# Two weight panels at a time behind a norm, and a residual's scaling moved among the next panels

## The chip, the cores and the metric

The kernel runs on one core of a Trainium2 chip. The time is the device time of one execution in microseconds (us). Three executions of the kernel before took 3048.42, 3040.75 and 3049.32 us; their median is 3048.42.

## What is computed

Two small language-model blocks run one behind the other on one sequence of 512 tokens of width 1024. The first has two layers, each a mixer (a linear recurrence with gated linear attention, then a forgetting attention) and an MLP, joined by layer norms; the second has two hybrid layers (three kinds of attention side by side, then a gated feed-forward), joined by RMS norms. What matters here is what stands around each norm:

```python
# first block, for both layers
x = layer_norm(ALPHA * x + gate * y, ln_g[layer, 0], ln_b[layer, 0])
shift, scale, gate = ada_mod(c, ada_w[layer, 1], ada_b[layer, 1])
u = x * (1.0 + scale) + shift
y = jnp.square(jax.nn.relu(u @ mlp_w1[layer] + mlp_b1[layer])) @ mlp_w2[layer] + mlp_b2[layer]
x = layer_norm(ALPHA * x + gate * y, ln_g[layer, 1], ln_b[layer, 1])

# second block, for both layers
h = rms_norm_2(x, norm_mix) * (1 + sc_m) + sh_m
... = jnp.split(h @ w_in, points, axis=-1)        # then the mixer
h = rms_norm_2(x, norm_ffn) * (1 + sc_f) + sh_f
gate, up = jnp.split(h @ w_gate_up, 2, axis=-1)
return x + gt_f * ((jax.nn.silu(gate) * up) @ w_down)
```

## The kernel before

**Layout.** Activations lie transposed: a matrix of 1024 features by 512 tokens is 8 tiles of 128 partitions by 512. `X` (residual) holds x. A product's input is kept as two tiles in the fast fp32 matmul format, `UHI` (in_high, the rounded value) and `ULO` (in_low, what rounding left). A weight panel is 1024 rows by 128 columns (512 KB) and is likewise split into `WHI` and `WLO`. `gemm` (from L585) multiplies one panel with all 8 input tiles into one PSUM bank: for each tile three matmuls of 128x512, high by high, high by low input, low weight by high (L596 to L598), so 24 for a panel. Products alternate between banks 0 and 1, and a product may start once the product two before it has been read out of its bank.

**Weights.** SyncE streams all panels in the order of use into a ring of 4 slots. ScalarE makes the high part (`high`, L1717), VectorE the low part (`low`, L1092), into 3 split slots; a slot is free when the matmuls of the panel three before are done. `prepare(ahead(key))` stands ahead of each panel's own work on both engines and splits the panels up to the second one after it. Among the MLP's panels the stream also holds rows of the modulation matrices ("ada"), about one a panel, which VectorE multiplies and sums (L1101).

**A norm.** PE sums the squares (or centred squares) with a constant matrix; ScalarE takes the inverse root into `R`, which is the first of two `tmp` tiles (L1759, L1762). Then `norm_split` makes the next product's input, tile by tile, for k = 0 to 7: VectorE scales X[k] into a stage tile (L1185), ScalarE adds the shift and rounds to in_high (L1800), VectorE takes what is left as in_low (L1182). The first panel behind the norm waits for in_low of each tile in turn (the `ready` argument of `gemm`); the second panel starts when the first has ended. There are seven such places: three layer norms (0 and 2 ahead of an MLP, 1 ahead of the forgetting attention) and, in both hybrid layers, an RMS norm ahead of the mixer and one ahead of the feed-forward. 

**Behind a layer norm** VectorE then scales all 8 tiles of the residual itself with gain and R (L1175) before it goes on to the MLP's panels. ScalarE's first step in the MLP waits for that (`s.wait_ge(*at("ln_norm", i - 1, KT - 1))`), since it writes the first panel's result into the tile that R lies in; it waits there before `evict`, so also before it splits the next weight panel. In the MLP each of the 16 panels of a half goes: ScalarE adds the bias and takes relu (L1731), VectorE squares (L1212), ScalarE rounds (L1810), VectorE takes the low part (L1202).

The order on each engine is the order of the calls in `tensor_program`, `vector_program` and `scalar_program`; semaphores alone tie them together.

## Time and profile before

| | us |
|---|---|
| median of three executions | 3048.42 (3040.75 to 3049.32) |
| the profiled execution, its own time | 3052.84 |
| its span, first to last instruction | 3051.4 |
| PE (TensorE matmul) busy | 2859.7, 94% of the span |
| VectorE (DVE) busy | 1673.2, 55% |
| ScalarE (ACT) busy | 1121.3, 37% |
| mean granted TensorE clock | 0.962 of full |

In the profile PE is the matmul unit and PEld its weight load, which runs beside it; L596 is line 596 of the kernel before. A timeline row gives start, duration, engine, line, operation, output<-inputs, and in brackets the idle time before it and what ended that. The duration of a matmul includes its way through the array: successive matmuls overlap, and the distance from start to start is what each costs. The granted clock is a share of full speed; PE has two levels, 1.2 and 2.4 GHz, so a mean of 0.9 over a stretch is a fifth of its time at the low one.

### The profile page before, as it was taken

Reading aid. Unit: us, or ns where it says so; the run is one execution under the profiler, and the core shown is the slowest. Engines: PE = TensorE matmul, PEld = TensorE weight load, DVE = VectorE, ACT = ScalarE, POOL = GpSimd, SP = SyncE. Lnnn points to the kernel's source line nnn. Section 1 sums busy time; section 2 is a strip of 40 time slices with the busy share of each in tenths; the row PEclk is TensorE's granted clock in tenths of the full one; section 3 lists DMA queues with packets and bytes.
Section 4 is the critical chain, followed back from the end, with each engine's and each line's share of the span. In section 5 each row is a group of like instructions: output and inputs, shape, how many; then the busy total and the mean of one; then the engine's idle time right before and its main releaser. Section 6 shows DMA issues by size and latency. Waiting matters only on the chain.

```text
span 3051.4 us, 35357 instructions
## 1 busy us (share of the span) xinstructions
PE 2859.7 (94%) x14106; PEld 2287.4 (75%) x14106; DVE 1673.2 (55%) x2910; ACT 1121.3 (37%) x1908; POOL 9.4 (0%) x21
## 2 busy tenths in 40 slices
PE   5888999989998899997999989999989899899998
PEld 4666888866666688875887867888868778678887
DVE  6678646554555755655547655443545476543334
ACT  3444324234554433324435333222334343332223
POOL 0000000000000000000000000000000000000000
PEclk9999999999998999998989899999999999999999
DMA  6345555522221465642220013444422100122222
GB/s 238 117 135 169 191 168 186 192 98 70 70 70 57 137 207 180 206 152 82 90 76 1 1 42 118 138 148 136 163 95 100 51 1 1 62 84 97 97 97 83
DMA packets 92067, 336.19 MB, mean 110 GB/s; under 512 B 10480, under 2 KB 10736, under 8 KB 91776
## 3 DMA queue, kind: packets, MB, share of 16 engines
q1 hardware_dynamic: 86800, 315.40, 30.7%
q10 hardware_dynamic: 3792, 14.31, 1.3%
q0 software_dynamic: 1312, 4.23, 0.5%
q8 instruction: 113, 1.85, 0.2%
q14 instruction: 50, 0.41, 0.0%
HBM read 331.76 MB, written 2.13 MB: 109 GB/s over the span
## 4 chain that ended last, share of the span: by engine, by line
PE 87%; DVE 7%; ACT 4%; DMA 1%; issue 1%; ACTq 0%; DVEq 0%
PE bank L596 22%; PE bank L597 22%; PE bank L598 22%; PE bank L781 2%; PE bank L795 2%; PE bank L770 2%; PE bank L1014 1%; DVE in_low L1182 1%; DVE hidden L1185 1%; PE bank L869 1%; PE bank L613 1%; PE bank L614 1%; PE bank L644 1%; PE bank L615 1%; PE bank L1022 1%; PE bank L1025 1%
## 5 line engine op out<-in xcount | busy, mean ns | idle before, releaser
L596 PE MATMUL bank<-in_high,weights_high 128*128 128x512 f32 x2160 | 874.6, 405 | 49.5 <-DVE in_low L1182 36.6
L597 PE MATMUL bank<-in_low,weights_high 128*128 128x512 f32 x2160 | 854.9, 396 | 0.0
L598 PE MATMUL bank<-in_high,weights_low 128*128 128x512 f32 x2160 | 854.2, 395 | 0.0
L1092 DVE TENSOR_TENSOR weights_low<-weight_ring,weights_high 128x1024 fp32r<-128x1024 f32 x404 | 494.1, 1224 | 469.8 <-ACT weights_high L1717 469.7
L1717 ACT ACTIVATE weights_high<-weight_ring 128x1024 fp32r<-128x1024 f32 x404 | 424.6, 1051 | 473.4 <-PE bank L598 320.6
L596 PEld LDWEIGHTS bank<-in_high,weights_high 128*128 128x128 f32 x2160 | 413.9, 192 | 186.1 <-issue 55.5
L598 PEld LDWEIGHTS bank<-in_high,weights_low 128*128 128x128 f32 x2160 | 413.8, 192 | 89.0
L597 PEld LDWEIGHTS bank<-in_low,weights_high 128*128 128x128 f32 x2160 | 414.9, 192 | 85.3 <-issue 4.1
L596 PE MATMUL bank<-hidden_split,weights_high 128*128 128x512 f32 x864 | 336.1, 389 | 0.0
L597 PE MATMUL bank<-hidden_split,weights_high 128*128 128x512 f32 x864 | 336.1, 389 | 0.0
L598 PE MATMUL bank<-hidden_split,weights_low 128*128 128x512 f32 x864 | 336.1, 389 | 0.0
L1101 DVE CUSTOM_DVE_ANT_0 weight_ring<-weight_ring,silu_c,vectors 128x1024 f32<-128x1024 f32 x192 | 244.4, 1279 | 3.4 <-DMA weight_ring<-stream 3.3
L596 PEld LDWEIGHTS bank<-hidden_split,weights_high 128*128 128x128 f32 x864 | 162.2, 188 | 33.8
L598 PEld LDWEIGHTS bank<-hidden_split,weights_low 128*128 128x128 f32 x864 | 162.2, 188 | 33.8
L597 PEld LDWEIGHTS bank<-hidden_split,weights_high 128*128 128x128 f32 x864 | 162.2, 188 | 33.5
L1810 ACT ACTIVATE hidden_split<-tmp 128x512 fp32r<-128x512 f32 x108 | 68.4, 633 | 262.5 <-DVE tmp L1546 205.5
L1731 ACT ACTIVATE tmp<-bank 128x512 f32<-128x512 f32 (+1 forms) x77 | 46.0, 597 | 245.1 <-PE bank L598 245.1
L1927 ACT ACTIVATE probs<-probs,columns 128x256 f32<-128x256 f32 (+4 forms) x144 | 73.7, 513 | 167.1 <-DVE columns L1346 164.8
L1202 DVE TENSOR_TENSOR hidden_split<-tmp,hidden_split 128x512 fp32r<-128x512 f32 x108 | 74.8, 693 | 75.5 <-ACT hidden_split L1810 75.5
L1546 DVE TENSOR_TENSOR tmp<-bank,tmp 128x512 f32<-128x512 f32 x44 | 30.4, 692 | 118.2 <-PE bank L598 118.2
L1731 ACT ACTIVATE tmp<-bank,vectors 128x512 f32<-128x512 f32 (+1 forms) x65 | 44.6, 686 | 136.2 <-PE bank L598 136.2
L781 PE MATMUL bank<-probs_T,hidden 128*64 128x128 f32 (+1 forms) x816 | 71.5, 302 | 24.4 <-DVE probs_T L1376 24.2
(332 smaller groups left out, 2961.4 us busy)
## 6 DMA issues: line engine op xcount, KB each, us to landing
weight_ring<-stream SPq DMA_DIRECT2D x597, 512.0 KB, 3.4
mixer_out<-cmp ACTq DMA_DIRECT2D x6, 1024.0 KB, 4.8
hidden<-forget_rows POOLq DMA_DIRECT2D x16, 256.0 KB, 3.8
residual<-x ACTq DMA_DIRECT2D x4, 512.0 KB, 12.7
mixer_out<-cmp SPq DMA_DIRECT2D x2, 1024.0 KB, 6.3
out<-mixer_out ACTq DMA_DIRECT2D x4, 512.0 KB, 2.7
constants<-consts ACTq DMA_DIRECT2D x1, 2013.5 KB, 21.0
silu_c<-c ACTq DMA_DIRECT2D x2, 512.0 KB, 4.6
```

The source lines that it names most:

```text
L596: pe.matmul(bank[:, :], WHI[:, z, cols], high, start=(k == 0), stop=False)
L597: pe.matmul(bank[:, :], WHI[:, z, cols], low, start=False, stop=False)
L598: ins = pe.matmul(bank[:, :], WLO[:, z, cols], high, start=False, stop=(k == ktiles - 1))
L770: pe.matmul(B[2 + z][:, 0:w], it["q"], it["k"], start=True, stop=True).then_inc(*mark("tensor_attention", *name, "scores", 2 * d + z))
L781: ins = pe.matmul(it["out"], it["v"][c], turned[:, blk(c)], start=it["start"] and c == 0, stop=it["stop"] and c == m - 1, skip_group_check ...
L1092: v.tensor_tensor(WLO[:, z, :], ring[:, n % RING, :], WHI[:, z, :].bitcast(F32), ALU.subtract).then_inc(*mark("weights_low", "low", n))
L1101: v.tensor_tensor_reduce(w, w, SC[:, :], 1.0, vec1("ada_b", col, col + 1), ALU.mult, ALU.add, MODS[:, col:col + 1]).then_inc(*mark("modula ...
L1202: v.tensor_tensor(HSPLIT[:, 1, at_, :], tmp, HSPLIT[:, 0, at_, :].bitcast(F32), ALU.subtract).then_inc(*mark("vector_mlp", *event))
L1717: s.activation(WHI[:, i % NSPLIT, :], ring[:, n % RING, :], ACT.Copy).then_inc(*mark("weights_high", "high", n))
L1731: s.activation(dst, view(B_of(key)[:, :]), func, **kw).then_inc(*mark("scalar_evict", "evicted", key))
L1810: s.activation(HSPLIT[:, 0, at_, :], tmp, ACT.Copy).then_inc(*mark("scalar_mlp", *event))
L1927: s.activation(p, p, ACT.Exp, bias=nm, scale=-1.0, accum_out=COL[:, c + 2 + z:c + 3 + z]).then_inc(*mark(sem, *name, "exp", i))
```

## The change

A new `gemm_pair` multiplies two panels with the same input tiles, into two banks. It waits at its start for both panels' low parts, then takes tile k for the first panel and tile k-2 for the second, in turns, waiting for in_low of tile k only ahead of the first panel's three matmuls. It stands behind six of the seven norms: for the first two "up" panels of each MLP, the first two rotary panels of each mixer, and the first gate and up panel of each feed-forward. The panel behind layer norm 1 stays as it was.

For layer norms 0 and 2 the inverse root goes to `M[:, 7, :]` instead of R, ScalarE no longer waits for `ln_norm` in the MLP, and the eight scalings of the residual are issued one at a time behind the first eight panels of the MLP's first half (`ln_scale`). Layer norms 1 and 3 keep theirs.

```diff
@@ -398,6 +398,8 @@
     ident, ones = const("ident"), const("ones")
     EPS = {1e-5: const("eps")[:, 0:1], 1e-6: const("eps")[:, 1:2]}
     R = TMP[:, 0, 0:T]
+
+    ln_root = lambda i: M[:, 7, :] if i in (0, 2) else R
     LNG, LNS, RB = (COL[:, 88 + 8 * z:96 + 8 * z] for z in range(3))
     blk = lambda b: slice(b * P, b * P + P)
     chunk = lambda c: slice(c * 64, c * 64 + 64)
@@ -600,6 +602,26 @@
                 ins.then_inc(*mark("panels_used", "used", n))
             ev.also("panels_used", "gemm", key)
 
+        def gemm_pair(keys, x, ready):
+
+            banks, used = [gemm_bank(key) for key in keys], [PANELS[key][0] for key in keys]
+            for n in used:
+                pe.wait_ge(*at("low", n))
+            for k in range(KT + 2):
+                for bank, n, j in zip(banks, used, (k, k - 2)):
+                    if not 0 <= j < KT:
+                        continue
+                    if j == k:
+                        pe.wait_ge(*at(*ready(k)))
+                    z, cols = split_turn[n] % NSPLIT, slice(j * P, j * P + P)
+                    high, low = x(j)
+                    pe.matmul(bank[:, :], WHI[:, z, cols], high, start=(j == 0), stop=False)
+                    pe.matmul(bank[:, :], WHI[:, z, cols], low, start=False, stop=False)
+                    ins = pe.matmul(bank[:, :], WLO[:, z, cols], high, start=False, stop=(j == KT - 1))
+                    if j == KT - 1:
+                        ins.then_inc(*mark("panels_used", "used", n))
+                        ev.also("panels_used", "gemm", keys[used.index(n)])
+
         def gemm_tok(name, panels, per, width, event, banks):
 
             for i in range(panels):
@@ -660,8 +682,10 @@
 
         def mlp(l, i):
             for half in range(2):
-                for j in range(HALF):
-                    gemm(("up", l, half, j), u_split, ready=lambda k: ("norm_out", "ln", i - 1, k) if (half, j) == (0, 0) else None)
+                if half == 0:
+                    gemm_pair([("up", l, 0, 0), ("up", l, 0, 1)], u_split, lambda k: ("norm_out", "ln", i - 1, k))
+                for j in range(2 if half == 0 else 0, HALF):
+                    gemm(("up", l, half, j), u_split)
                 for m in range(KT):
                     gemm(("down", l, half, m), h_split, HALF, ready=lambda k: hidden_ready(("up_low", l, half), HALF, k) if m == 0 else None)
             ln_mean(i)
@@ -872,8 +896,9 @@
 
             conv = lambda m: gemm(("conv", l, m), u_split)
             z = lambda m: gemm(("z", l, m), u_split)
-            gemm(ropes[0], u_split, ready=lambda k: ("norm_out", "mix", l, k))
-            for i in range(1, 5):
+            gemm_pair(ropes[0:2], u_split, lambda k: ("norm_out", "mix", l, k))
+            turn(0)
+            for i in range(2, 5):
                 gemm(ropes[i], u_split)
                 turn(i - 1)
             gemm(("kc", l), u_split)
@@ -945,8 +970,11 @@
             for a in range(0, FF2_T, HALF):
                 tiles = min(HALF, FF2_T - a)
                 for j in range(a, a + tiles):
-                    gemm(("gate", l, j), u_split, ready=lambda k: ("norm_out", "ffn", l, k) if j == 0 else None)
-                    gemm(("gup", l, j), u_split)
+                    if j == 0:
+                        gemm_pair([("gate", l, 0), ("gup", l, 0)], u_split, lambda k: ("norm_out", "ffn", l, k))
+                    else:
+                        gemm(("gate", l, j), u_split)
+                        gemm(("gup", l, j), u_split)
                 for m in range(KT):
                     gemm(("fdown", l, a, m), h_split, tiles, 
                                ready=lambda k: hidden_ready(("gup_low", l), tiles, k, a) if m == 0 else None)
@@ -1170,19 +1198,23 @@
                 v.wait_ge(*last("modulations"))
             v.wait_ge(*at("ln_r", i))
             if mod is not None:
-                norm_split(("ln", i), lambda k: LNG[:, k:k + 1], lambda k: LNS[:, k:k + 1])
-            for k in range(KT):
-                v.scalar_tensor_tensor(X[:, k, :], X[:, k, :], gcol_[:, k:k + 1], R, ALU.mult, ALU.mult).then_inc(
-                    *mark("vector_norm", "ln_norm", i, k))
-
-        def norm_split(event, gain, shift):
+                norm_split(("ln", i), lambda k: LNG[:, k:k + 1], lambda k: LNS[:, k:k + 1], ln_root(i))
+            if i in (1, 3):
+                for k in range(KT):
+                    ln_scale(i, k, gcol_)
+
+        def ln_scale(i, k, gcol_):
+            v.scalar_tensor_tensor(X[:, k, :], X[:, k, :], gcol_[:, k:k + 1], ln_root(i), ALU.mult, ALU.mult).then_inc(
+                *mark("vector_norm", "ln_norm", i, k))
+
+        def norm_split(event, gain, shift, root):
 
             def tile_low(k):
                 v.wait_ge(*at("norm_high", *event, k))
                 v.scalar_tensor_tensor(ULO[:, k, :], H[:, STAGE + k, :], shift(k), UHI[:, k, :].bitcast(F32), ALU.add,
                                        ALU.subtract).then_inc(*mark("vector_norm", "norm_out", *event, k))
             for k in range(KT):
-                v.scalar_tensor_tensor(H[:, STAGE + k, :], X[:, k, :], gain(k), R, ALU.mult, ALU.mult).then_inc(
+                v.scalar_tensor_tensor(H[:, STAGE + k, :], X[:, k, :], gain(k), root, ALU.mult, ALU.mult).then_inc(
                     *mark("vector_norm", "norm_scaled", *event, k))
                 if k:
                     tile_low(k - 1)
@@ -1190,7 +1222,7 @@
 
         def rms_norm(event, gain, shift):
             v.wait_ge(*at("rms_r", *event))
-            norm_split(event, lambda k: gain[:, k:k + 1], lambda k: shift[:, k:k + 1])
+            norm_split(event, lambda k: gain[:, k:k + 1], lambda k: shift[:, k:k + 1], R)
 
         def input_low(k, src, high, event):
             v.wait_ge(*at(*high))
@@ -1211,6 +1243,8 @@
                     v.wait_ge(*at("evicted", key))
                     v.tensor_tensor(h, h, h, ALU.mult).then_inc(*mark("vector_mlp", "up_square", l, half, j))
                     hidden_low(j, h, ("up_high", l, half, j), ("up_low", l, half, j))
+                    if half == 0 and j < KT:
+                        ln_scale(i - 1, j, vec1("ln_g", 8 * i - 8, 8 * i))
                 if half == 0:
                     gb = COL[:, 72:80]
                     v.wait_ge(*last("modulations"))
@@ -1785,7 +1819,7 @@
                 s.wait_ge(*at("ln_centre", i, k))
                 s.activation(M[:, k, :], X[:, k, :], ACT.Square).then_inc(*mark(sem, "ln_square", i, k))
             s.wait_ge(*at("ln_var", i, KT - 1))
-            inv_sqrt(sem, B[3], 1e-5, R, ("ln_r", i))
+            inv_sqrt(sem, B[3], 1e-5, ln_root(i), ("ln_r", i))
             if mod is not None:
                 s.wait_ge(*at("ln_shift", i))
                 norm_high(("ln", i), LNS)
@@ -1815,8 +1849,6 @@
                     h = TMP[:, j % 2, 0:T]
                     if j > 1:
                         s.wait_ge(*at("up_low", l, half, j - 2))
-                    elif j == 0 and half == 0:
-                        s.wait_ge(*at("ln_norm", i - 1, KT - 1))
                     b1 = 32 * l + HALF * half + j
                     evict(("up", l, half, j), h, ACT.Relu, bias=vec1("mlp_b1", b1, b1 + 1))
                     s.wait_ge(*at("up_square", l, half, j))
```

On PE, at the MLP behind layer norm 0, the matmuls of input tiles 2 and 3 (bank0 is the first panel's, bank1 the second's; "vector_norm" is the wait for in_low). Before:

```order
L596 MATMUL bank0<-in_high_49,weights_high 128x512 [waits vector_norm]
L597 MATMUL bank0<-in_low,weights_high 128x512
L598 MATMUL bank0<-in_high_49,weights_low 128x512
L596 MATMUL bank0<-in_high_49,weights_high 128x512 [waits vector_norm]
L597 MATMUL bank0<-in_low,weights_high 128x512
L598 MATMUL bank0<-in_high_49,weights_low 128x512
```

Now:

```order
L618 MATMUL bank0<-in_high_49,weights_high 128x512 [waits vector_norm]
L619 MATMUL bank0<-in_low,weights_high 128x512
L620 MATMUL bank0<-in_high_49,weights_low 128x512
L618 MATMUL bank1<-in_high_49,weights_high 128x512
L619 MATMUL bank1<-in_low,weights_high 128x512
L620 MATMUL bank1<-in_high_49,weights_low 128x512
L618 MATMUL bank0<-in_high_49,weights_high 128x512 [waits vector_norm]
```

Between two tiles of the first panel there now stand three matmuls of the second.

On VectorE, at the same place, from the last two in_low tiles on (L1101 or L1129 is a modulation row, "ISA" its two parts; weights_low the next panel's low part; tmp and hidden_split the first panel's square and low part). Before:

```order
L1182 SCALAR_TENSOR_TENSOR in_low<-hidden,columns,in_high_49 128x512 [waits scalar_norm] x2
L1175 SCALAR_TENSOR_TENSOR residual<-residual,vectors1,tmp 128x512 x8
L1101 ISA weight_ring,modulations<-weight_ring,silu_c,vectors1 128x1024 [waits panel_landed_0]
L1101 ISA modulations 128x1
L1092 TENSOR_TENSOR weights_low<-weight_ring,weights_high 128x1024 [waits weights_high]
L1212 TENSOR_TENSOR tmp<-tmp 128x512 [waits scalar_evict]
L1202 TENSOR_TENSOR hidden_split_51<-tmp,hidden_split_51 128x512 [waits scalar_mlp]
```

Now:

```order
L1214 SCALAR_TENSOR_TENSOR in_low<-hidden,columns,in_high_49 128x512 [waits scalar_norm] x2
L1129 ISA weight_ring,modulations<-weight_ring,silu_c,vectors1 128x1024 [waits panel_landed_0]
L1129 ISA modulations 128x1
L1120 TENSOR_TENSOR weights_low<-weight_ring,weights_high 128x1024 [waits weights_high]
L1244 TENSOR_TENSOR tmp<-tmp 128x512 [waits scalar_evict]
L1234 TENSOR_TENSOR hidden_split_51<-tmp,hidden_split_51 128x512 [waits scalar_mlp]
L1207 SCALAR_TENSOR_TENSOR residual<-residual,vectors1,mixer_out 128x512
L1129 ISA weight_ring,modulations<-weight_ring,silu_c,vectors1 128x1024 [waits panel_landed_2]
```

The eight scalings are gone from behind the last in_low, and one stands behind the low part of each of eight panels.

On ScalarE, at the same place, the last in_high tiles and the MLP's first steps. Before:

```order
L1800 ACTIVATE in_high_49<-hidden,columns 128x512 [waits vector_norm] x7
L1717 ACTIVATE weights_high<-weight_ring 128x1024 [waits panels_used,panel_landed_1,vector_norm]
L1731 ACTIVATE tmp<-bank0,vectors1 128x512 [waits panels_used]
L1810 ACTIVATE hidden_split_51<-tmp 128x512 [waits vector_mlp]
L1717 ACTIVATE weights_high<-weight_ring 128x1024 [waits panels_used,panel_landed_3]
```

Now:

```order
L1834 ACTIVATE in_high_49<-hidden,columns 128x512 [waits vector_norm] x7
L1751 ACTIVATE weights_high<-weight_ring 128x1024 [waits panels_used,panel_landed_1]
L1765 ACTIVATE tmp<-bank0,vectors1 128x512 [waits panels_used]
L1844 ACTIVATE hidden_split_51<-tmp 128x512 [waits vector_mlp]
L1751 ACTIVATE weights_high<-weight_ring 128x1024 [waits panels_used,panel_landed_3]
```

The order is the same; the high part of the third panel has lost its wait for VectorE ("vector_norm").

## Rows read from the trace of the kernel before

**Rows 1.** The page: busy time of PE and of its weight load

```profile
PE 2859.7 (94%) x14106; PEld 2287.4 (75%) x14106; DVE 1673.2 (55%) x2910; ACT 1121.3 (37%) x1908; POOL 9.4 (0%) x21
```

**Rows 2.** Waits over the whole span: us in total, times, longest

```profile
PE bank L596 <- DVE in_low L1182: 36.6, 25, 7.3
```

**Rows 3.** Timeline of PE, first MLP: first panel, second panel, start of the third

```profile
266.96 0.47 PE L596 MATMUL bank<-in_high,weights_high 128*128 128x512 f32 x1 [4.00 <-DVE in_low L1182]
...
268.19 0.71 PE L596 MATMUL bank<-in_high,weights_high 128*128 128x512 f32 x1 [0.30 <-DVE in_low L1182]
...
269.54 0.77 PE L596 MATMUL bank<-in_high,weights_high 128*128 128x512 f32 x1
270.11 0.63 PE L597 MATMUL bank<-in_low,weights_high 128*128 128x512 f32 x1
270.53 0.63 PE L598 MATMUL bank<-in_high,weights_low 128*128 128x512 f32 x1
...
274.81 0.50 PE L596 MATMUL bank<-in_high,weights_high 128*128 128x512 f32 x1 [0.36 <-DVE in_low L1182]
...
275.69 0.50 PE L596 MATMUL bank<-in_high,weights_high 128*128 128x512 f32 x1
...
276.49 0.40 PE L596 MATMUL bank<-in_high,weights_high 128*128 128x512 f32 x1
...
281.72 0.39 PE L598 MATMUL bank<-in_high,weights_low 128*128 128x512 f32 x1
283.44 0.47 PE L596 MATMUL bank<-in_high,weights_high 128*128 128x512 f32 x1 [1.33 <-DVE weights_low L1092]
```

**Rows 4.** Timeline of VectorE at the same place

```profile
272.69 0.75 DVE L1182 SCALAR_TENSOR_TENSOR in_low<-hidden,columns,in_high 128x512 fp32r<-128x512 f32 x1
...
274.01 1.62 DVE L1182 SCALAR_TENSOR_TENSOR in_low<-hidden,columns,in_high 128x512 fp32r<-128x512 f32 x2
275.56 5.38 DVE L1175 SCALAR_TENSOR_TENSOR residual<-residual,vectors,tmp 128x512 f32<-128x512 f32 x8
280.86 1.28 DVE L1101 CUSTOM_DVE_ANT_0 weight_ring<-weight_ring,silu_c,vectors 128x1024 f32<-128x1024 f32 x1
...
282.07 1.23 DVE L1092 TENSOR_TENSOR weights_low<-weight_ring,weights_high 128x1024 fp32r<-128x1024 f32 x1
```

**Rows 5.** Timeline of ScalarE at the same place

```profile
274.13 0.72 ACT L1800 ACTIVATE in_high<-hidden,columns 128x512 fp32r<-128x512 f32 x1 [0.60 <-DVE hidden L1185]
280.97 1.06 ACT L1717 ACTIVATE weights_high<-weight_ring 128x1024 fp32r<-128x1024 f32 x1 [6.12 <-DVE residual L1175]
281.94 0.67 ACT L1731 ACTIVATE tmp<-bank,vectors 128x512 f32<-128x512 f32 x1
```

**Rows 6.** Six windows, from the first panel's start to the third's; last columns clock, DMA, GB/s

```profile
266.96:283.44 16.48, 14.12 (x48) 9.34 (x49) 16.35 (x25) 5.98 (x8) 0.00 (x0) 0.90 0.02 5
1008.17:1024.66 16.49, 13.94 (x48) 9.25 (x49) 16.36 (x25) 5.98 (x8) 0.00 (x0) 0.90 0.01 3
1395.44:1410.43 14.99, 14.63 (x48) 10.28 (x49) 9.78 (x14) 5.90 (x8) 0.00 (x0) 0.80 0.10 37
1849.87:1864.85 14.98, 14.45 (x48) 10.15 (x49) 12.20 (x17) 8.13 (x10) 0.00 (x0) 0.81 0.24 76
2223.13:2238.12 14.99, 14.16 (x48) 9.80 (x49) 9.78 (x14) 5.89 (x8) 0.00 (x0) 0.85 0.10 35
2675.85:2690.84 14.99, 14.48 (x48) 10.16 (x49) 11.01 (x15) 8.12 (x10) 0.00 (x0) 0.81 0.19 56
```

**Rows 7.** Timeline of PE in the first product, which takes four banks in turn

```profile
31.05 0.40 PE L631 MATMUL bank<-in_high,weights_low 128*128 128x512 f32 x1
31.29 0.39 PE L629 MATMUL bank<-in_high,weights_high 128*128 128x512 f32 x1
31.52 0.39 PE L630 MATMUL bank<-in_low,weights_high 128*128 128x512 f32 x1
```

**Rows 8.** Timeline of VectorE among the MLP's later panels

```profile
322.52 0.69 DVE L1212 TENSOR_TENSOR tmp<-tmp 128x512 f32<-128x512 f32 x1 [1.01 <-ACT tmp L1731]
```

**Rows 9.** PE's waits from the third panel to the next norm's sums (window 283.4 to 625)

```profile
PE bank L644 <- ACT mixer_out L1786: 1.4, 1, 1.4
```

## The prediction

> **What bounds the kernel now.** I read the page's busy times first: PE works for 94% of the span [rows 1], so time can only come from the places where it stands still or runs slow. The list of waits names the one that this change is about: 36.6 us in 25 waits for in_low of a norm [rows 2]. Not all of it can go. Seven of the waits, one for each norm, are the wait for the first tile (4.00 us at the first MLP [rows 3]); the chain of sums, root and first tile ahead of it is not touched. What can go stands behind the first tile, and for that I read the three engines' timelines at the first MLP.
>
> The input's tiles come every 1.32 us: two in_low on VectorE start at 272.69 and 274.01 [rows 4], since between them stands the next tile's scaling. A tile of one panel costs PE three matmuls. The starts of successive ones are 0.42 to 0.43 us apart at the low clock (270.11 to 270.53 [rows 3]) and 0.23 at the full one (31.29 to 31.52 [rows 7]; 0.227 over the 24 matmuls from 276.49 to the end 0.23 behind the start at 281.72 [rows 3], 5.45 us a panel). So at the low clock a tile costs 1.28 us and PE is just filled; at full clock it costs 0.68 and PE waits about half the time, as at 274.81 [rows 3]. The first panel thus ends at 276.49 and only then does the second begin, with all its input there. That is the second panel's 5.45 us, nearly all of it behind the last tile.
>
> At the MLPs there is a second loss. VectorE scales the residual for 5.38 us from 275.56 [rows 4]; ScalarE waits for that for 6.12 us before it splits the third panel's high part [rows 5], VectorE's modulation row and low part follow [rows 4], and PE, done with the second panel at 281.95, starts the third at 283.44 [rows 3]: 1.49 us.
>
> **The change, part by part.** *The pair.* Tiles 0 and 1 go as before. From tile 2 on, each tile brings six matmuls: 1.36 us at full clock, more than the 1.32 between tiles, and 2.56 at the low one. So from there PE should not wait again. What is left of the 48 matmuls is 42, or 42 x 0.227 = 9.53 us at full clock. Tile 2 begins 2.58 us behind tile 0 at the first MLP (269.54 less 266.96 [rows 3]); I take 2.6 at all six. Each us of low clock behind that point costs 1 - 0.227/0.427 = 0.47 us. The low clock's length is in the windows' granted clock [rows 6], each window running from the first panel's start to what follows the second: twice (1 - clock) times the length. That gives 3.3 us at both MLPs, 6.0, 5.7, 4.5 and 5.7 at the other four. At the first MLP PE had run the first tile at full clock and was slow from tile 1 (0.43 between starts from 269.54 on, and by 276.49 long fast [rows 3]), so 3.3 us end some 1.9 behind tile 2; I take that at both. At the others the first matmuls are already slow, and 3.4, 3.1, 1.9 and 3.1 us lie behind tile 2.
>
> The pair's end, counted from the first start: 2.6 + 9.53 + 0.47 x slow = 13.0 at the MLPs, and 13.7, 13.6, 13.0 and 13.6 at mixer, feed-forward, mixer, feed-forward. Against the window lengths of 16.48, 16.49, 14.99, 14.98, 14.99 and 14.99 [rows 6] that is 3.46, 3.47, 1.26, 1.38, 1.97 and 1.39 us less: together 12.9. The MLPs' figures take in the 1.49 us wait each, which the next step has to earn.
>
> *The scaling moved.* VectorE ends its last in_low at about 275.6, the modulation row and the low part (1.28 and 1.23 [rows 4]) then end at 278.1. ScalarE is free for the high part from 274.9 [rows 5]. The pair ends at about 280.0, so the third panel is ready 1.9 us early, and the 1.49 us go. The fourth panel is the tight one. The first panel ends at about 278.0 (three tiles, 2.04 us, ahead of the pair's end). From there: eviction 0.7, square 0.7, high part 0.7, low part 0.7, the moved scaling 0.67 (5.38/8), modulation row 1.28, weights' low part 1.2: about 6.1 us, done at 284.1; PE asks for it at 280.0 + 5.45 = 285.5. It is 1.4 us early. Later VectorE does 4.3 us of that chain plus 0.67 for each 5.45 us panel, and it idles 1.01 us in each before the square [rows 8], so eight scalings fit.
>
> *What costs nothing.* The pair needs both panels' low parts and both banks at its start; all four were ready long before, since VectorE splits the second panel while the projection ahead still runs, and cover is the 4 us wait for the first tile itself. The banks change every three matmuls: the first product does so with four banks at 0.23 us a start [rows 7]. The root in a `mixer_out` tile is written and read in the same lengths. Behind the pair PE meets no wait for weights up to the next norm's sums, one of 1.4 us for a square apart [rows 9], so nothing is in place to take the gain back, and everything behind is shifted as it stands.
>
> The Trainium skill's page "TensorE: Matmul & The Clock Gate" (section "Back-to-back issue gap") gives 216 ns for a matmul of 512 columns at full clock; the rows show 227. By the page's figure each pair would end 42 x 0.011 = 0.46 us sooner, an estimate of 2.8 us more in all; the measurement decides and the sum stays.
>
> **The sum** is 12.9 us. Bounds: with no slow stretch at all behind tile 2 the six pairs give 2.8 us each (14.99 - 2.6 - 9.53) and the MLPs' waits 3.0, near 20; with the low clock 2 us longer at each and the MLPs' waits staying, 12.9 - 5.6 - 3.0 = 4.3. From the profiled execution's 3052.84 this makes 3039.9, from the median of 3048.42 it makes 3035.5. A change of 0.3% is 9.1 us; that is about what a measurement can tell from none here, the three runs lying 8.6 us apart.
>
> **The rivals.** *A: a new wait in the MLP.* If the fourth panel comes late (a ring slot landing late, or ScalarE and VectorE waiting for each other once more than in my chain), PE waits there, and since each of eight panels carries one scaling, the moved 5.4 us could come back one by one. For it: only 1.4 us of margin. Against: 1.01 us of idle a panel [rows 8], and low parts that are done nearly two panels ahead once PE is the slower. Price: the MLPs give 1 to 2 us each in place of 3.5, total gain 8, 3040: within 0.3%.
>
> *B: the low clock lasts longer in the pair.* PE would drain the backlog at 0.43 a matmul. Two us more at each place cost 5.6: gain 7, 3041. Against it: PE was already filled at the low clock before, so what it does up to the clock's rise is the same.
>
> *C: it ends earlier,* as the windows differ by 1.5 us among themselves [rows 6]: gain 16 to 19, 3031.
>
> *D, slower.* The pair changes banks every three matmuls; if that broke the stream into pieces, the clock could stay low for the whole pair: 42 x 0.427 = 17.9 in place of 9.5, an end at 20.5. Against 15.0 and 16.5 that loses 5.5 us at four places and 4.0 at two, 30 us: 3078. It decides from 4.6 us more low clock at each place (12.9/6/0.47). Against it: four banks in turn ran at full clock [rows 7]. The same page (section "A second HAM failure mode: psum-queue depth-cycling") tells of a kernel in which cycling through PSUM banks let the clock swing between its levels; there PE idled between groups. The trace shows the cycling without the swing.
>
> *E: nothing shows,* as the gain is within what runs differ by.
>
> **How the numbers follow.** My forecast (gain 10 to 16) has 0.70, A 0.10, B 0.08, C 0.06, D 0.03, E 0.03. Faster by over 0.3% takes the forecast and C: 0.76; within 0.3% A, B and E: 0.21; slower 0.03. The time is the forecast's 3035.5. The range takes in 6 us of gain at one end (A and B) and 19 at the other (C), 3029 to 3043.
>
> **What would show it.** Right: at six places, the matmuls of the pair without a wait from tile 2 on, the third panel's start 13.0 to 13.7 us behind the first's in place of 15.0 to 16.5; waits of PE for in_low down by about 4 us (the starts behind the first tile); ScalarE's 6.12 us wait for the residual gone; no wait of PE for weights_low at the MLPs. Wrong: L596's successor waiting for weights_low or a ring transfer in the MLP's panels 3 to 10 (A), starts 0.43 us apart past 6 us behind the first (B, D), or the gain present at the six places and the same time found as new waits before the end.

## The result

Nine executions of each: the changed kernel took 3026.02 us in the median (3023.30 to 3035.70), the kernel before 3046.57 (3036.19 to 3049.57). The medians lie 20.6 us apart; the ratio of the executions is put at 0.9945, 95% interval 0.993 to 0.996, which is 17 us less (12 to 21). A second comparison, six executions against 25, gave 3030.43 us in the median and 0.9951 (0.9932 to 0.9969), 15 us less. Faster, as forecast, by somewhat more than the 12.9 us of the sum; the first median lies 3 us under the low end of the range.

The profiled execution has a span of 3024.3 us against 3051.4. The page's busy times, and PE's waits over the whole span (answering to [rows 1, 2]):

```profile
PE 2842.2 (94%) x14106; PEld 2279.3 (75%) x14106; DVE 1672.9 (55%) x2910; ACT 1122.6 (37%) x1908; POOL 9.4 (0%) x21
```

```profile
PE bank L618 <- DVE in_low L1214: 27.3, 8, 6.9
...
PE bank L598 <- DVE in_low L1214: 5.0, 4, 4.0
```

Waits for in_low fell from 36.6 to 32.3 us. What is left is the first tile's at seven places, and little more: the six pairs (L618) have 8 waits in all.

PE at the first MLP (answering to [rows 3]):

```profile
265.39 0.47 PE L618 MATMUL bank<-in_high,weights_high 128*128 128x512 f32 x1 [4.00 <-DVE in_low L1214]
...
268.07 0.68 PE L618 MATMUL bank<-in_high,weights_high 128*128 128x512 f32 x1
...
269.40 0.59 PE L618 MATMUL bank<-in_high,weights_high 128*128 128x512 f32 x1
269.82 0.40 PE L619 MATMUL bank<-in_low,weights_high 128*128 128x512 f32 x1
...
278.49 0.39 PE L598 MATMUL bank<-in_high,weights_high 128*128 128x512 f32 x1
```

Tile 2 starts at 268.07 and no matmul waits from there to the third panel (L598), which starts at 278.49, 13.10 us behind the first, where it was 16.48.

VectorE and ScalarE there (answering to [rows 4, 5]):

```profile
272.45 1.63 DVE L1214 SCALAR_TENSOR_TENSOR in_low<-hidden,columns,in_high 128x512 fp32r<-128x512 f32 x2
274.00 1.28 DVE L1129 CUSTOM_DVE_ANT_0 weight_ring<-weight_ring,silu_c,vectors 128x1024 f32<-128x1024 f32 x1
...
275.21 1.22 DVE L1120 TENSOR_TENSOR weights_low<-weight_ring,weights_high 128x1024 fp32r<-128x1024 f32 x1
...
279.37 0.75 DVE L1207 SCALAR_TENSOR_TENSOR residual<-residual,vectors,mixer_out 128x512 f32<-128x512 f32 x1
...
281.24 1.22 DVE L1120 TENSOR_TENSOR weights_low<-weight_ring,weights_high 128x1024 fp32r<-128x1024 f32 x1
282.38 0.69 DVE L1244 TENSOR_TENSOR tmp<-tmp 128x512 f32<-128x512 f32 x1
```

```profile
273.20 1.04 ACT L1751 ACTIVATE weights_high<-weight_ring 128x1024 fp32r<-128x1024 f32 x1
276.65 0.69 ACT L1765 ACTIVATE tmp<-bank,vectors 128x512 f32<-128x512 f32 x1 [2.40 <-PE bank L620]
```

ScalarE's 6.12 us wait is gone. The third panel's low part is done at 276.4, 2.1 us early; the fourth's at 282.5, where PE asks for it at 278.49 + 5.45 = 283.9: 1.5 us early.

The six windows, from the first panel's start to what follows the pair (answering to [rows 6]; the last three columns are clock, DMA share, GB/s):

```profile
265.39:278.49 13.10, 12.80 (x49) 9.91 (x49) 11.60 (x17) 6.39 (x9) 0.00 (x0) 0.87 0.14 48
1006.24:1019.24 13.00, 12.70 (x49) 9.90 (x49) 11.59 (x17) 6.39 (x9) 0.00 (x0) 0.87 0.17 45
1389.90:1402.25 12.35, 12.35 (x49) 9.79 (x50) 9.78 (x14) 5.91 (x8) 0.00 (x0) 0.88 0.10 28
1834.18:1847.87 13.69, 13.69 (x48) 10.72 (x49) 11.25 (x17) 8.14 (x10) 0.00 (x0) 0.79 0.17 48
2205.76:2218.11 12.35, 12.35 (x49) 9.75 (x50) 9.78 (x14) 5.91 (x8) 0.00 (x0) 0.89 0.10 32
2650.00:2663.71 13.71, 13.71 (x48) 10.71 (x49) 10.05 (x15) 8.13 (x10) 0.00 (x0) 0.79 0.12 39
```

The places gain 3.38, 3.49, 2.64, 1.29, 2.64 and 1.28 us: 14.7 in all. The two spans differ by 27.1. Where the other 12 came from is the question of half the experiments. Most of them lie in stretches of the hybrid layers that hold no changed instruction. A first guess was that they are therefore not the change's; that does not follow yet, since a change can alter what comes behind it.

### The profile page after: what moved, and what is told of

The parts are those of the page before. It is cut to its first block, busy times and chain, and to the rows that moved or that the text cites. A ratio compares the mean times of both kernels' runs of the same rounds, so it can differ in the third digit from the quotient of the medians.

```text
span 3024.3 us, 35357 instructions
## 1 busy us (share of the span) xinstructions
PE 2842.2 (94%) x14106; PEld 2279.3 (75%) x14106; DVE 1672.9 (55%) x2910; ACT 1122.6 (37%) x1908; POOL 9.4 (0%) x21
## 4 chain that ended last, share of the span: by engine, by line
PE 89%; DVE 5%; ACT 4%; DMA 1%; issue 1%; ACTq 0%; DVEq 0%
PE bank L598 22%; PE bank L599 22%; PE bank L600 22%; PE bank L819 2%; PE bank L794 2%; PE bank L805 2%; PE bank L1042 1%; PE bank L635 1%; PE bank L1050 1%; PE bank L893 1%; PE bank L636 1%; PE bank L666 1%; PE bank L637 1%; PE bank L618 1%; PE bank L1053 1%
## 5 line engine op out<-in xcount | busy, mean ns | idle before, releaser
L598 PE MATMUL bank<-in_high,weights_high 128*128 128x512 f32 x2064 | 826.3, 400 | 15.4 <-DVE in_low L1229 7.4
L600 PE MATMUL bank<-in_high,weights_low 128*128 128x512 f32 x2064 | 812.4, 394 | 0.0
L599 PE MATMUL bank<-in_low,weights_high 128*128 128x512 f32 x2064 | 811.7, 393 | 0.0
L598 PEld LDWEIGHTS bank<-in_high,weights_high 128*128 128x128 f32 x2064 | 393.2, 190 | 128.7 <-issue 24.0
L599 PEld LDWEIGHTS bank<-in_low,weights_high 128*128 128x128 f32 x2064 | 392.8, 190 | 83.4 <-issue 4.1
L600 PEld LDWEIGHTS bank<-in_high,weights_low 128*128 128x128 f32 x2064 | 392.1, 190 | 83.5
L598 PE MATMUL bank<-hidden_split,weights_high 128*128 128x512 f32 x864 | 336.1, 389 | 0.0
L1129 DVE CUSTOM_DVE_ANT_0 weight_ring<-weight_ring,silu_c,vectors 128x1024 f32<-128x1024 f32 x192 | 244.5, 1279 | 3.7 <-DMA weight_ring<-stream 3.6
L598 PEld LDWEIGHTS bank<-hidden_split,weights_high 128*128 128x128 f32 x864 | 162.2, 188 | 33.7
```

Source lines behind the costliest of these rows:

```text
L598: pe.matmul(bank[:, :], WHI[:, z, cols], high, start=(k == 0), stop=False)
L599: pe.matmul(bank[:, :], WHI[:, z, cols], low, start=False, stop=False)
L600: ins = pe.matmul(bank[:, :], WLO[:, z, cols], high, start=False, stop=(k == ktiles - 1))
L1129: v.tensor_tensor_reduce(w, w, SC[:, :], 1.0, vec1("ada_b", col, col + 1), ALU.mult, ALU.add, MODS[:, col:col + 1]).then_inc(*mark("modula ...
```

## The experiments

The experiments ran on three chips, each beside the kernel before on the same chip. Its medians there were 3045.50, 3042.70 and 3048.36 us, so whole times are compared by ratios to it, or within one chip. Five kernels ran once, for their trace, and are read by their stages.

**The two parts apart.** The scaling moved, without pairs:

```diff
         def gemm_pair(keys, x, ready):
+            gemm(keys[0], x, ready=ready)
+            gemm(keys[1], x)
+
+        def gemm_pair_unused(keys, x, ready):
```

> The scaling moved and ScalarE's wait gone, but the first two panels one after the other at all seven norms. Both theories of the change's parts: the third panel at the two MLPs starts 15.0 us behind the first (16.48 before, 13.0 to 13.1 with the whole change), since its low part is ready before the second panel ends; the four hybrid places stay at 15.0. Gain 1.5 us at each MLP, 3.0 in all, so within 0.1 to 0.2% of the kernel before. If the changed kernel's surplus over its six places (27 us in span against 14.7 us at the places) came from the moved scaling, this one would be 12 us or more faster as well.

The pairs, with the scaling as before:

```diff
-    ln_root = lambda i: M[:, 7, :] if i in (0, 2) else R
+    ln_root = lambda i: R
...
-            if i in (1, 3):
-                for k in range(KT):
+            for k in range(KT):
...
-                    if half == 0 and j < KT:
-                        ln_scale(i - 1, j, vec1("ln_g", 8 * i - 8, 8 * i))
...
+                    elif j == 0 and half == 0:
+                        s.wait_ge(*at("ln_norm", i - 1, KT - 1))
```

> The six pairs, but with the scaling in one piece behind the norm, the root in the tmp tile and ScalarE's wait as before. Theory of the two parts needing each other at the MLPs: VectorE ends the scaling and the third panel's low part at the same time as before, so the third panel still starts 16.4 to 16.5 us behind the first and the MLPs gain nothing, though the pair ends at 13.1; the four hybrid places give 5 to 8 us by how long the low clock lasts. Total gain 5 to 8 us from the places. Rival (the parts add up independently): third panel at 14.6 behind the first, 1.9 us at each MLP, total 9 to 12.

PE at the first MLP, first tile and third panel, with the scaling moved:

```profile
264.66 0.47 PE L598 MATMUL bank<-in_high,weights_high 128*128 128x512 f32 x1 [4.00 <-DVE in_low L1218]
...
279.65 0.39 PE L598 MATMUL bank<-in_high,weights_high 128*128 128x512 f32 x1
```

and with the pairs alone:

```profile
263.39 0.47 PE L618 MATMUL bank<-in_high,weights_high 128*128 128x512 f32 x1 [4.00 <-DVE in_low L1213]
...
276.15 0.39 PE L620 MATMUL bank<-in_high,weights_low 128*128 128x512 f32 x1
279.87 0.47 PE L598 MATMUL bank<-in_high,weights_high 128*128 128x512 f32 x1 [3.33 <-DVE weights_low L1120]
```

14.99 and 16.48 us, as expected of both. The pair alone ends 13.0 us behind its start (276.15 + 0.23) and then waits 3.33 us for the weights: at the MLPs it is worth nothing without the moved scaling, which alone is worth 1.5, and together they give 3.4 to 3.5. Over the whole, the scaling moved gave 0.9992 (0.9975 to 1.0009), which 3.0 us at its two places fit and 12 us would not, and the pairs alone 0.9976 (0.9961 to 0.9991), 7 us, with 7.6 at its four hybrid places. The rival for each is out.

**How much margin the moved scaling has.** Two more scalings beside each of the eight, whose results are not read:

```diff
                     if half == 0 and j < KT:
+                        for d in range(2):
+                            v.scalar_tensor_tensor(M[:, 3 + d, :], X[:, j, :], vec1("ln_g", 8 * i - 8 + j, 8 * i - 7 + j),
+                                                   ln_root(i - 1), ALU.mult, ALU.mult).then_inc(*step("vector_norm"))
                         ln_scale(i - 1, j, vec1("ln_g", 8 * i - 8, 8 * i))
```

> The changed kernel with two more scalings of the same size (their results are not read) beside each of the eight in each MLP. It measures the margin of the moved scaling. By the trace of the changed kernel VectorE takes 5.00 us for a panel with one scaling while it catches up, PE 5.45; each further scaling adds 0.67. Theory 'VectorE's chain is the only limit': 6.3 us a panel, 0.9 over PE's, the fourth panel's low part has 1.5 us of margin and loses 1.3 of it at once, so PE waits in each of the following panels by up to 0.9 us: 5 to 7 us in each MLP, first wait of PE for weights_low at the fourth or fifth panel. Rival 'low parts are made far ahead, there is ample cover': no wait of PE, the MLP takes 365.7 us as with one scaling.

From one norm's sums to the next, the first MLP took 370.9 us in place of 365.8 and the second 372.0 in place of 365.7, 5.1 and 6.3 more. PE's waits from 262 to 380:

```profile
PE bank L598 <- DVE weights_low L1120: 3.4, 6, 0.6
```

and VectorE's low parts of the first and second panel's output, with the two added scalings (L1248) between them:

```profile
278.73 0.69 DVE L1234 TENSOR_TENSOR hidden_split<-tmp,hidden_split 128x512 fp32r<-128x512 f32 x1 [0.70 <-ACT hidden_split L1847]
279.33 1.41 DVE L1248 SCALAR_TENSOR_TENSOR mixer_out<-residual,vectors,mixer_out 128x512 f32<-128x512 f32 x2
...
285.05 0.69 DVE L1234 TENSOR_TENSOR hidden_split<-tmp,hidden_split 128x512 fp32r<-128x512 f32 x1 [0.70 <-ACT hidden_split L1847]
```

VectorE's round for a panel takes 6.32 us (278.73 to 285.05), its 0.70 us of waiting for ScalarE included; with one scaling it took 5.01 (277.37 to 282.38 in the changed kernel). PE meets six waits in the first MLP, the first at the fifth panel, and its panels then start 6.32 us apart instead of 5.44. So the limit of the moved scaling is reached when VectorE's round for a panel passes PE's 5.45. The single execution took 3035.98 us.

**The lag.** Both panels on the same tile:

```diff
-            for k in range(KT + 2):
-                for bank, n, j in zip(banks, used, (k, k - 2)):
+            for k in range(KT):
+                for bank, n, j in zip(banks, used, (k, k)):
...
-                    if j == k:
+                    if n == used[0]:
```

> The changed kernel with both panels of a pair on the same tile in place of two tiles apart. Theory 'PE is the bound of the pair from its first filled tile on, so the lag only decides what is left at the end': at the MLPs PE also works in the gap behind tile 0, so the last matmul of the pair ends 0.3 to 0.6 us sooner (12.5 against 13.0); at the hybrid places PE is filled at the low clock either way, so no difference there beyond the clock's own. But the first panel now ends 0.7 us ahead of the second's end in place of 2.0, and the third panel needs its bank, which ScalarE reads for 0.6 to 0.7 us behind it: a new wait of 0.2 to 0.4 us ahead of the third panel, which takes back about half. Rival 'the lag costs nothing and brings nothing': the third panel at 13.0 at the MLPs and no wait.

```profile
277.65 0.39 PE L620 MATMUL bank<-in_high,weights_low 128*128 128x512 f32 x1
278.14 0.50 PE L598 MATMUL bank<-in_high,weights_high 128*128 128x512 f32 x1
```

The first start was at 265.27, so the pair ends 12.61 us behind it (277.65 + 0.23). The third panel starts at 12.87, 0.26 us later: ScalarE reads its bank out from 277.40 to 278.09. At the second MLP it is 12.82. With the lag it was 12.9 to 13.1, so up to 0.2 us is left of the 0.4 that the pair gains, and the wait takes the rest back. At the hybrid places it is 12.48, 13.84, 13.59 and 13.87: nothing gained. The single execution took 3039.59 us.

**Is the surplus the change's?** The changed kernel and the kernel before, unaltered, once more each, for a second trace (3028.45 and 3045.28 us):

> The changed kernel once more, for a second trace. Theory 'the surplus is how the low stretches of PE's clock fall, which differs between executions': the stretches between the six places (the hybrid mixers, the attention stages) show another granted clock than in the first trace whenever the time differs, with 0.47 us for each us more of low clock, and times from 3023 to 3036 as in the nine runs. The pair's own length is 12.3 to 13.8 us at each place again, longer where the low clock lasts longer. Rival 'the surplus belongs to the change': the mixers take 191.5 us and the attention stages 174.9 again in every execution.

> The kernel before, for a second trace. Theory 'the surplus of the first comparison is how the low stretches of PE's clock fall': among the stretches without a pair (attention of the first block 280.5 to 283.8, hybrid mixers 174.4 to 177.7, hybrid attention stages 250.8 to 255.1 so far) at least one stands at another of these levels than in the first trace of before, while the MLPs take 369.2 and the feed-forwards 369.8 again. Rival 'each kernel has its own levels': the same lengths as in the first trace to 0.3 us.

And a delay of 1.6 us at one place, in both kernels:

```diff
             v.wait_ge(*at("rms_r", *event))
+            if event == ("mix", 0):
+                for d in range(2):
+                    v.scalar_tensor_tensor(H[:, STAGE, :], X[:, 0, :], gain[:, 0:1], R, ALU.mult, ALU.mult).then_inc(
+                        *step("vector_norm"))
+                    v.wait_ge(*last("vector_norm"))
```

> The changed kernel with two more scalings, one behind the other, ahead of the first tile at the first mixer alone, so that everything from there comes 1.4 to 1.6 us later. It asks what ends the low clock in a pair. In seven traces the first mixer's low clock ended 2.9 us behind the first start with a pair and 5.9 without. Theory 'the rise has its place against PE's earlier work': the low clock ends 1.3 to 1.5 us behind the start, and the pair takes 12.2 us or less. Rival 'it counts from the first matmul of the product': 2.9 us again and 12.35. Rival 'it falls where it falls': anything between, 12.2 to 13.9.

> The same two scalings ahead of the first mixer in the kernel before. The two panels take 15.0 us again, since the input's tiles pace them as long as the clock is up before the last tile. Theory 'the rise has its place against PE's earlier work': the low clock ends 4.4 us behind the first start instead of 5.9. Rival 'it counts from the first matmul': 5.9. In both cases the mixer and attention stretches may stand at another of their levels (174.4 to 179.3 and 250.6 to 257.3 us), as they differ between executions of one kernel.

Windows of the stretches that hold no pair: first a layer's mixer up to its first attention score, then its attention stage up to the sums of the next norm. Before, first layer and second:

```profile
1410.43:1588.09 177.66, 177.66 (x885) 148.72 (x883) 81.32 (x140) 61.06 (x99) 0.00 (x0) 0.93 0.27 92
1588.09:1843.22 255.13, 234.26 (x1638) 191.42 (x1638) 165.14 (x455) 109.40 (x304) 0.00 (x0) 0.93 0.05 18
```

Before once more, second layer:

```profile
2237.63:2410.54 172.91, 172.91 (x885) 144.58 (x883) 81.33 (x140) 61.05 (x99) 0.00 (x0) 0.96 0.28 95
2410.54:2661.62 251.08, 230.43 (x1637) 187.85 (x1637) 165.33 (x455) 109.20 (x304) 0.00 (x0) 0.95 0.06 18
```

Changed, first layer:

```profile
1402.25:1576.68 174.43, 174.43 (x886) 146.03 (x884) 81.34 (x140) 61.16 (x99) 0.00 (x0) 0.95 0.28 95
1576.68:1827.53 250.85, 230.17 (x1638) 187.57 (x1638) 165.35 (x455) 109.47 (x304) 0.00 (x0) 0.95 0.06 18
```

Changed, 1.6 us later, first layer:

```profile
1404.94:1584.21 179.27, 179.27 (x885) 150.00 (x883) 81.30 (x140) 61.05 (x99) 0.00 (x0) 0.92 0.27 91
1584.21:1841.41 257.20, 236.63 (x1637) 192.87 (x1637) 165.61 (x455) 109.35 (x304) 0.00 (x0) 0.92 0.06 18
```

Before, 1.6 us later, first layer:

```profile
1409.90:1582.77 172.87, 172.87 (x885) 144.46 (x883) 81.32 (x140) 61.08 (x99) 0.00 (x0) 0.96 0.28 95
1582.77:1833.64 250.87, 230.19 (x1637) 187.59 (x1637) 165.34 (x455) 109.30 (x304) 0.00 (x0) 0.95 0.06 18
```

In the mixer PE is busy all the time and has the same matmuls; what differs is the granted clock, and with it the length: 172.9, 174.5, 176.1, 177.7 or 179.3 us, the attention stage 250.6 to 251.1, 253.6 to 255.1 or 257.2. Several of these lengths turn up in kernels with pairs and without (172.9, 174.5 and 176.1 in the mixer, 250.6 to 251.1 and 254.7 to 255.1 in the attention stage); 177.7 stood only in kernels without pairs, 179.3 and 257.2 only in kernels with them. The two layers of one execution can differ, as in the second trace of before. So a difference of this size can come without any change of the kernel.

The first trace of before had both layers at the long attention level and the first of the changed kernel at the short, which makes 4.3 + 4.2, with 3.2 + 1.6 in the mixers: 13.3 us. The start of the kernel was 1.6 us shorter as well, and the first block's attention 3.1 longer (283.6 against 280.5, and the two traces of before differ there as well, 280.5 and 283.5), so 11.8 in all; with 15.3 for the change's own stretches that is the 27.1. The second pair of traces (spans 3043.8 and 3027.0) differs by 16.8, of which 13.6 at the MLPs and the four hybrid places. So the change is worth 13.6 to 15.3 us at its own places, counted stretch by stretch; what goes beyond, in these two pairs of traces, stands in stretches whose length follows the granted clock.

Whether the change makes the short lengths likelier is not shown. In the six traces with pairs two tiles apart, no delay and no unread matmuls, all twelve hybrid attention stages are short (250.6 to 251.1 us); with both panels on the same tile one of two is long. In the three traces without pairs and without the delay four of six are long (254.7 to 255.1), and in the delayed kernel before both are short again. The two comparisons, 15 and 17 us with an interval of 9 to 21 between them, leave little room for such an effect on average, but do not exclude a few us.

The delay does not settle it either. The delayed changed kernel took 3043.05 us and the delayed kernel before 3036.48, in one execution each, on a chip where the unaltered kernel before took 3033.75 to 3059.52 us in eleven: the second lies within what the kernel does by itself. The first lies above all 15 executions of the changed kernel, none of which is known to be from that chip; the long lengths in its trace (179.3 and 257.2) also stand in the second layer of the kernel without lag, which had no delay.

Nor did the delay say what ends the low clock in a pair. In the kernel before it ended 4.0 us behind the first start, not 5.9, near the 4.4 of the theory that PE's earlier work sets its place, and the two panels took 15.0 us again. In the changed kernel it ended at 4.7, neither at 1.4 nor at 2.9, and the pair took 13.2. Neither theory holds for both. That stays open.

**Keeping PE busy while it waits.** Matmuls nobody reads, ahead of each pair (14, at the two mixers 8 and 24):

```diff
-        def gemm_pair(keys, x, ready):
+        def gemm_pair(keys, x, ready, warm=14):
...
                 pe.wait_ge(*at("low", n))
+            z = split_turn[used[0]] % NSPLIT
+            for d in range(warm):
+                pe.matmul(B[4][:, :], WHI[:, z, 0:P], WHI[:, z, 512:1024], start=True, stop=True)
```

> The changed kernel with matmuls that nobody reads (two operands that are already there, into bank 4) while PE waits for the first tile of a norm at the six places: 14 of them, 8 ahead of the first mixer, 24 ahead of the second. Theory 'the low clock in the pair comes from PE's idle time ahead of it': the pair runs at full clock and ends 12.3 us behind its first start or a little later, 0.7 us sooner at the MLPs, 1.3 at the feed-forwards, 0 to 1 at the mixers: 3 to 5 us in all against the changed kernel. Rival 'the extra matmuls hold up the first tile': at the first mixer, where the clock is already low, 8 x 0.43 = 3.4 us fit in the 4.0 us wait, so no delay is expected; if they run late the first start moves by up to 2 us at a place and the kernel is no faster.

The first pair of the first feed-forward, from its first start to the third panel's, at full clock from end to end (clock 1.00 in place of 0.79):

```profile
1843.38:1855.70 12.32, 11.61 (x48) 8.96 (x49) 11.34 (x17) 8.13 (x10) 0.00 (x0) 1.00 0.09 27
```

So the low clock in a pair comes from PE's idle time ahead of it at these four places: the MLPs took 364.9 and 365.0 us in place of 365.7, the feed-forwards 367.05 each in place of 368.5; 4.4 us less on these four. At the mixers the low clock stayed in part, and the pairs took 13.4 and 12.9. The whole did not follow: 3032.44 us in the median (3025.37 to 3039.55), 0.9966 (0.9949 to 0.9982), against 3030.43 for the changed kernel on the same chip. In its trace the first mixer stood at 179.27 and the attention stages at 257.24 and 254.80, the long levels.

**The seventh place, and all together.** Behind layer norm 1 the 12 matmuls of a tile of the value panels stand behind tiles 2 and 4 of the forget panel; the next two panels are split ahead of the scalings:

```diff
+            for k in range(KT):
+                ...
+                if k in (2, 4):
+                    values(k // 2 - 1)
+            for j in range(2, KT):
+                values(j)
...
+            if i == 1:
+                prepare(ahead(("fl",)))
```

> The changed kernel with the seventh norm done likewise: behind layer norm 1 the matmuls of two input tiles of the value panels (12 a tile, into four banks) stand between those of the forget panel's later tiles, and both engines split the next two panels ahead of ScalarE's wait and VectorE's eight scalings. Theory 'the place, not the form, gives the gain': the third value panel starts 18 to 18.6 us behind the norm's first tile in place of 21.9, 3 to 3.5 us less from the norm's sums to the first attention score (91.4 us before and in the changed kernel). Rival 'the chain on VectorE behind the scalings (soft-plus and running sum of the forget gates, then the first rotated heads) sets the start of the attention': the stretch stays at 90 to 91.4.

> The seventh place together with the matmuls that keep PE busy at the six others. Local sum against the changed kernel: 3.5 us at the seventh place (87.9 in place of 91.4) and 4 to 5 at the six, as each was measured alone; if the sum over the parts holds and the levels of the stretches between fall as in the kernels so far, the median is 3018 to 3024 and below the seventh place alone (3023). Rival, from the one run with PE kept busy (3032 against 3026 to 3030 of the changed kernel): the busy matmuls move the clock's low stretches in the mixer and attention stages to their long levels, the local gain is given back there, and the median is 3024 to 3030.

> The changed kernel with the seventh place once more, on the same chip as the one above, so that the two can be compared. Expected 15 to 20 us below the kernel before, as the first time (ratio 0.9936).

The start of the norm's first tile and that of the third value panel, 72 matmuls later:

```profile
633.50 0.47 PE L845 MATMUL bank<-in_high,weights_high 128*128 128x512 f32 x1 [3.99 <-DVE in_low L1250]
...
652.02 0.39 PE L833 MATMUL bank<-weights_high,in_high 128*128 128x512 f32 x1
```

That is 18.5 us (18.3 in the second run), where the kernel before and the changed one have 22.0, and the stretch to the first attention score took 87.9 and 87.7 us, not 91.4: the place gives 3.5 us. Against the kernel before this version gave 0.9936 (0.9914 to 0.9959) and 0.990 (0.9873 to 0.9927), its ten executions 3016.73 to 3032.35. Its ratios are the lowest, though it never ran beside the changed kernel; the first one's interval overlaps the changed kernel's, the second one's does not. With PE kept busy as well the ratio was 0.9928 (0.9902 to 0.9954), with 3026.23 us in the median (3019.41 to 3032.46), where the seventh place alone took 3016.73 to 3018.86 on the same chip. In its trace the first attention stage stood at 257.28 and the first mixer at 176.1, against 250.8 and 174.5. That is as the rival had it, the local gain given back; one trace shows the lengths, not what set them.

## Why the prediction was right, and where it was not

- *The pair.* Right in kind: no wait from tile 2 on, and each us of low clock behind tile 2 costs about 0.47. With no low clock a pair took 12.3; with a low clock that ended 5.7 to 5.8 us behind the first start, 3.1 us behind tile 2, it took 13.7. Pair ends of 13.0, 13.0, 13.7, 13.6, 13.0 and 13.6 were forecast; 13.10, 13.00, 12.35, 13.69, 12.35 and 13.71 came. The term that was off is the low clock at the mixers: 6.0 and 4.5 us were carried over from before, and it lasted 2.9, so these two places gave 1.4 and 0.7 us more than the sum has; rival C, which was to give 16 to 19 us, came there and nowhere else. At the second mixer it varies: the pair took 12.35 and 13.56 in two traces of the same kernel, a gain of 2.6 or 1.4 us, so the 0.7 there is luck. At the first the low clock was short in all seven traces with pairs and nothing added ahead of them (until 2.8 to 3.4 us), long in all three without pairs or delay (5.7 to 6.1). In the changed kernel it ended 2.9 us behind the first start and the second panel's first matmul came at 3.5, so what decides it happens ahead of the matmuls that the change adds, and was not found.
- *The moved scaling.* The margin at the fourth panel was put at 1.4 and is 1.5, and the third panel's wait went. The two chains behind the margin agree a little less well: the prediction's terms from the first panel's end to the fourth's low part add up to 5.95 us, not to the 6.1 that it states, and the chain took 5.8 (276.65 to 282.46). Rival A did not come; with three scalings in place of one it does. That the MLP's two halves need each other was in the sum only as "which the next step has to earn"; the experiments show it.
- *Nothing costs anything.* Banks in turn ran at 0.23 us a start; rival D was not seen.
- *"Everything behind is shifted as it stands"* is the step that failed. It holds for PE's waits, not for the clock: the stretches behind stand at one of several lengths, which differ between executions of one kernel and made 11.8 us of the first two traces' difference. The range was built from the six places alone, with the executions' own spread of 13 us left out of its ends, so the median fell 3 us below it. The sum for the places, 12.9, is 0.7 to 2.4 us short of what they gave.

## What to carry to other kernels

Behind a norm whose output comes tile by tile at a fixed pace, let as many products share each tile as keep the matrix unit filled. Here two were enough: six matmuls take 1.36 us at full clock, and a tile comes every 1.32. The gain, 1.3 to 2.6 us at each hybrid place and 3.4 at the MLPs, is kept only if the next weights are ready when the pair ends. Read a change of this size at its places, stretch by stretch: a whole-kernel time mixes it with the clock's own differences, which here were as large.

## What was not expected

Executions of one kernel differ by 13 us and more, as much as this change brings, and in the traces the difference stands in stretches of fixed work whose length takes a few values. Matmuls that keep the clock up during a wait gave 0.7 us at each MLP and 1.45 at each feed-forward, and nothing that the whole could show.
